# A dilated attention mixer ordered by head pairs

## What is computed

```python
proj = (h @ w_in).reshape(B, S, 3, 3, 16, 64)      # 3 groups, each q, k, v of 16 heads
for gi, (window, dilation) in enumerate(((128, 1), (512, 4), (2048, 16))):
    q = rms_norm(proj[:, :, gi, 0], g_q[gi]); k = rms_norm(proj[:, :, gi, 1], g_k[gi])
    s = q . k * 64 ** -0.5 + bias_table[bucket(pos_k - pos_q)]     # -inf outside the window
    lse = logsumexp(s); o = exp(s - lse) @ v
wts = softmax(lses over the 3 groups)
y = sum(wts * o) @ w_o
x = x + gate1 * y
```

## Time and profile before

| | us |
|---|---|
| median of 3 runs | 2215.91 |
| the profiled execution | 2213.28 |
| its span, first to last instruction | 2211.5 |
| PE busy | 2029.5 (92%) |
| DVE busy | 1458.9 (66%) |
| ACT busy | 1085.9 (49%) |
| POOL busy | 172.1 (8%) |
| mean granted PE clock | 0.953 |

### The profile page before, as it was taken

How to read it: one execution, slowest core, us unless ns; L and a number is a source line. 1 busy time by engine, 2 the same in 40 slices (tenths; PEclk the granted TensorE clock), 3 DMA queues, 4 the chain that set the end, 5 groups by cost and what they waited for, 6 DMA issues and landing times.

```text
span 2211.5 us, 34384 instructions
## 1 busy us (share of the span) xinstructions
PE 2029.5 (92%) x14140; PEld 1868.4 (84%) x14140; DVE 1458.9 (66%) x2577; ACT 1085.9 (49%) x1674; POOL 172.1 (8%) x243
## 2 busy tenths in 40 slices
PE   2758999889999998999889989999999879999998
PEld 1746999789898978999888889999999767888886
DVE  6696885666766556754765553888886696555554
ACT  3544553325665144543555445444444695444444
POOL 3020000000000000000000000000000492000000
PEclk7879999889999699999999999999999999999999
DMA  6534687526554014665433434555555203555553
GB/s 263 188 124 153 202 283 249 172 75 212 199 173 157 20 39 143 193 189 181 162 126 120 139 114 162 185 186 191 182 184 188 96 1 125 190 190 186 187 190 124
DMA packets 97084, 356.22 MB, mean 161 GB/s; under 512 B 10704, under 2 KB 10832, under 8 KB 96544
## 3 DMA queue, kind: packets, MB, share of 16 engines
q1 hardware_dynamic: 83824, 305.04, 41.1%
q0 software_dynamic: 12672, 48.08, 7.0%
q10 hardware_dynamic: 432, 0.90, 0.1%
HBM read 352.93 MB, written 1.05 MB: 160 GB/s over the span
## 4 chain that ended last, share of the span: by engine, by line
PE 79%; DVE 14%; ACT 4%; DMA 1%; issue 1%; SPq 0%; POOL 0%; DVEq 0%; ACTq 0%
PE psum L386 22%; PE psum L387 22%; PE psum L388 22%; PE psum L379 12%; DVE C L1432 2%; PE psum L393 1%; DVE wl L1460 1%; DVE araw L1443 1%; DVE one L1432 1%; ACT work L945 1%; DVE one L1437 1%; DVE work L1440 1%; DMA first<-in_ada_w 1%; ACT sqh L945 0%; DVE first L1443 0%
## 5 line engine op out<-in xcount | busy, mean ns | idle before, releaser
L1460 DVE TENSOR_TENSOR wl<-raw,wh 128x1024 fp32r<-128x1024 f32 (+1 forms) x564 | 686.7, 1223 | 469.8 <-ACT wh L957 468.7
L957 ACT ACTIVATE wh<-raw 128x1024 fp32r<-128x1024 f32 (+1 forms) x564 | 593.0, 1053 | 461.2 <-PE psum L388 444.7
L386 PE MATMUL psum<-peer_hh,wh 128*128 128x256 f32 x1152 | 325.9, 283 | 4.1 <-DVE peer_hl L1432 4.0
L387 PE MATMUL psum<-peer_hl,wh 128*128 128x256 f32 x1152 | 324.9, 282 | 0.0
L388 PE MATMUL psum<-peer_hh,wl 128*128 128x256 f32 x1152 | 324.9, 282 | 0.0
L386 PEld LDWEIGHTS psum<-peer_hh,wh 128*128 128x128 f32 x1152 | 218.2, 189 | 5.4 <-issue 4.4
L387 PEld LDWEIGHTS psum<-peer_hl,wh 128*128 128x128 f32 x1152 | 218.4, 190 | 0.0
L388 PEld LDWEIGHTS psum<-peer_hh,wl 128*128 128x128 f32 x1152 | 218.3, 189 | 0.0
L386 PE MATMUL psum<-wh,csh 128*128 128x512 f32 x512 | 202.5, 396 | 0.0
L387 PE MATMUL psum<-wl,csh 128*128 128x512 f32 x512 | 202.5, 395 | 0.0
L388 PE MATMUL psum<-wh,csl 128*128 128x512 f32 x512 | 202.5, 395 | 0.0
(11 more groups left out here) (422 smaller groups left out, 4589.2 us busy)
## 6 DMA issues: line engine op xcount, KB each, us to landing
raw<-in_mlp_w SPq DMA_DIRECT2D x128, 512.0 KB, 4.2
raw<-in_eu SPq DMA_DIRECT2D x128, 512.0 KB, 3.2
raw<-in_ev SPq DMA_DIRECT2D x128, 512.0 KB, 3.2
araw<-in_ada_w POOLq DMA_DIRECT2D x80, 512.0 KB, 4.2
raw<-in_dil_qk SPq DMA_DIRECT2D x48, 512.0 KB, 4.1
raw<-in_dil_v SPq DMA_DIRECT2D x24, 512.0 KB, 4.4
first<-in_ada_w SPq DMA_DIRECT2D x8, 1024.0 KB, 18.2
raw<-in_w_in SPq DMA_DIRECT2D x16, 512.0 KB, 3.3
```

The lines of the kernel that those rows point to most:

```text
L386: e.matmul(o, l[0], r[0], start=start, stop=False, skip_group_check=loose)
L387: e.matmul(o, l[0], r[1], start=False, stop=False, skip_group_check=loose)
L957: e.activation(b.wh[v % NSPLIT][:, 0:cols], b.raw[v % NRAW][:, 0:cols], ACT.Copy).then_inc(S.hi, 1)
L1460: e.tensor_tensor(b.wl[v % NSPLIT][:, 0:cols], b.raw[v % NRAW][:, 0:cols], b.wh[v % NSPLIT][:, 0:cols].bitcast(F32), ALU.subtract).then_in ...
```

## The change

The order of all engines is one list, `DIL_ORDER`, from which `PLAN` takes its units too.

- The value units come first, 18 of 24 (those for heads 0 to 11), and both bias tables are made beside them; `B` holds both tiles, and the mask is loaded in one piece.
- Then the q and k units in eight rounds, one for each pair of heads c: six units (q and k of three groups), so that a bank holds q and k of one group. `qk` keeps two rounds.
- The norm of round c is split: squares, sums and means in the round; the three reciprocal roots together one round later, after unit 3 (`root`), with the root squares and DVE's refining and scaling after units 3 and 4. DVE scales q and k separately, 256 columns each.
- The four attention steps of pair c-2 stand in round c, two after unit 0 and two after unit 1. `work` has three score buffers and one for transposed probabilities; in a step PE does `s3` before `s2`, and ACT the copy before the exponential.
- The last six value units follow round 7, beside the last scalings. Steps 24 and 25 come after them, steps 26 to 34 between the first six units of the output projection.
- The output projection goes by rows: unit i takes slice i of the attention output and adds to all eight column blocks in four banks, so it can begin when pair 0 is done; the residual is added after the last unit's blocks, and the four squares and sums follow.
- Modulation steps: one after every fourth of the 18 value units, then three in each round and in the late values (31 in all; before, every fourth unit and every third attention step).

```diff
+def dil_order():
+    values = [("dil_v", 8 * g + x, x // 2) for g in range(3) for x in range(8)]
+    out = []
+    for i, e in enumerate([e for e in values if e[2] < 3]):
+        out.append(e)
+        if i % 4 == 3:
+            out.append(("tick", 0, 0))
+    out.append(("biased", 0, 0))
+    late = [e for e in values if e[2] == 3]
+    def beside(c, z):
+        if z % 2 == 0:
+            s, g = (c, z // 2 - 1) if z else (c - 1, 2)
+            if 0 <= s < 8:
+                out.append(("sum", s, g))
+        s, g = {3: (c, 0), 5: (c, 1), 0: (c - 1, 2)}.get(z, (-1, 0))
+        if c and z == 3:
+            out.append(("root", c - 1, 0))
+        if c and z in (3, 4):
+            out.append(("root square", c - 1, z - 3))
+        if c and z == 4:
+            out.append(("root square", c - 1, 2))
+        if 0 <= s < 8:
+            out.append(("mean", s, g))
+        if z % 2 and c < 8:
+            out.append(("square", c, z // 2))
+        if z in (0, 2, 3):
+            out.append(("tick", c, z))
+        if c and z in (3, 4):
+            out.append(("scale", c - 1, z - 3))
+        if c and z == 4:
+            out.append(("scale", c - 1, 2))
+        for u in {0: (4 * c - 8, 4 * c - 7), 1: (4 * c - 6, 4 * c - 5)}.get(z, ()):
+            if 0 <= u < 24:
+                out.append(("step", u, 0))
+    for c in range(8):
+        for z in range(6):
+            out.append(("dil_qk", 8 * z + c, z))
+            beside(c, z)
+    for z in range(6):
+        out.append(late[z])
+        beside(8, z)
+    out += [("step", 24, 0), ("step", 25, 0)]
+    tail = [(26,), (27,), (28, 29), (30, 31), (32, 33), (34,), (), ()]
+    for i, steps in enumerate(tail):
+        out += [("step", u, 0) for u in steps] + [("dil_w_o", i, 0)]
+    return out
...
 # ScalarE
+            elif kind == "root":
+                ac.wait_ge(S.act, n[0])
+                if i:
+                    ac.wait_ge(S.dve, at["dqk", "out", i - 1, 2])
+                for g in range(3):
+                    act(m.hrs[:, g, :], m.hms[:, (3 * i + g) % 4, :], ACT.Abs_reciprocal_sqrt, mark=("root", i, g))
...
 # VectorE
+        def head_norm(c, g):
+            sq, ms, y = m.hrq[g], m.hms[:, (3 * c + g) % 4, :], m.hrs[:, g, :]
+            ve.wait_ge(S.act, at["head rs0", c, g])
+            stt(sq, ms, -0.5, sq, ALU.mult, ALU.mult)
+            own()
+            stt(sq, sq, 1.5, y, ALU.add, ALU.mult)
...
+            for x, gain in enumerate(("dil_g_q", "dil_g_k")):
+                z = slice(256 * x, 256 * x + 256)
+                stt(m.qk[:, c % 2, 2 * g + x, :], ps[:, z], vc(b, gain, g), sq[:, z], ALU.mult, ALU.mult,
+                    mark=("dqk", "out", c, g))
...
 # TensorE, the output projection
+        def rows(i):
+            if i == 0:
+                for c2 in range(4):
+                    take("dil_o", c2)
+            j = weights("dil_w_o", i)
+            pe.wait_ge(S.dve, at["dil", "out", i])
+            for c in range(8):
+                o = b.psum[:, at["bank", "dil_o", c // 2], (c % 2) * 256:(c % 2) * 256 + 256]
...
+        for c2 in range(4):
+            give("dil_o", c2, sem=S.dve, key=("dil_o", "out", c2))
+            square_sums("dil_o", c2, m.work)
```

More of the change, by code:

```diff
@@ L145, in plan @@
     add("mlp_w2", 32)
[L146 to L149, removed]
+    for kind, i, j in DIL_ORDER:
+        if kind in ("dil_v", "dil_qk", "dil_w_o"):
+            add(kind, 1, first=i)
     add("mlp_w1", 32, first=32)
@@ L686, in dilated @@
         phase("dil")
[L687 to L731, removed]
-                give("dv", g, c2, sem=S.act, key=("dv", "out", g, c2))
@@ L770, in s3, with step @@
                    mark=("dil", "pv", u) if kb == 3 else None)
[L771 to L777, removed]
+            if u % 4 == 3:
+                give("do", c, sem=S.dve, key=("dil", "out", c))
+        def step(i):
             if i < 32:
                 s1(i)
+            if 0 <= i - 3 < 32:
+                s3(i - 3)
@@ new lines, in dilated @@
+        for kind, i, z in DIL_ORDER:
+            if kind == "dil_v":
+                values(i, z)
+                next(side, None)
+            elif kind == "biased":
+                for _ in side:
+                    pass
+            elif kind == "dil_qk":
+                c = i % 8
+                if z % 2 == 0:
+                    take("dqk", c, z // 2)
+                ps = b.psum[:, at["bank", "dqk", c, z // 2], (z % 2) * 256:(z % 2) * 256 + 256]
+                j = weights("dil_qk", i)
+                for k in range(8):
+                    mm3(ps, wsp(j, k * 128, 128), sp(m.hh, k), k == 0, k == 7, unit=k == 7)
+            elif kind == "sum":
+                head_sums(i, z)
+            elif kind == "scale":
+                give("dqk", i, z, sem=S.dve, key=("dqk", "out", i, z))
+            elif kind == "step":
+                step(i)
+            elif kind == "dil_w_o":
+                rows(i)
@@ L1156, in dilated @@
         _, shift = shift_gain(b, 1, 0)
-        norm_x("n2", ("mlp0", 2), shift, m.hh, m.work[:, 0:2048], m.work[:, 2048:2816])
+        norm_x("n2", ("mlp0", 2), shift, m.hh, m.work[:, 0:2048], m.vtf[:, 0:768])
         ac.wait_ge(S.dve, at["tab diff"])
         act(m.tabs[0], m.ot[:, 0:192], ACT.Copy, mark=("tabs", "hi"))
[L1160 to L1200, removed]
@@ L1218, in mixer2 @@
+        for c2 in range(4):
+            square("dil_o", c2, m.work, ("dil_o", "out", c2))
     def mixer2():
@@ L2208, in modulation @@
                 yield
+            groups[0] = first + count
             yield
+    groups = [16]
     mods = modulation()
@@ L2218, in tick, with mod_until @@
                 next(mods, None)
+    def mod_until(first):
+        while groups[0] <= first:
+            next(mods)
     def lows(tag, m):
```

261 lines of the change are left out of this document (162 added, 99 removed).

## The result

The changed kernel took 2177.95 us (median of 4 runs, 2176.93 to 2178.57) against 2215.23 for the one before on the same chip (4 runs, 2213.45 to 2216.1): ratio 0.9832, 95% interval 0.9815 to 0.9849. The forecast was 2179, its range 2163 to 2199. The profiled execution took 2178.34 us with a span of 2176.5.

What follows compares the result with a forecast made beforehand. PE bounds the mixer, partly at half clock: 795.0 + 9 + 2 + 1 + 6.6 + 2 = 815.6, + 8.8 = 824.4 instead of 861.3; 36.9 less gives 2176.4 profiled, 2179 us median, range 2163 to 2199.

Steps and rivals of the forecast that it cites:

- first mixer matmul to first bias matmul: Mixer start: first comparison comes one 1.2 us operation sooner, so bias work starts at 426.7; before, PE waited until 427.85.
- clock in the bias stage, and the seam: Bias tables beside eighteen value units: 9 us lost to half clock (bounds 0 and 16), 2 waiting after the last group.
- rounds 0 to 7: Query and key rounds: 1 us of waits for rounds 0 and 1, 6.6 for rounds 2 to 7 (bounds 0 and 18).
- late values and tail: After the rounds: round 8 needs no new wait; copies in the three last steps cost 2 us, bounds 1 and 5.
- last output issue to the MLP: Mixer end: adds start within the last unit, 8.8 us in all, 7.2 before; over 9 would show it wrong.
- PE's sum: Whole mixer at full clock: units, bias matmuls, head sums and steps total 368.3 us; last output matmul issued at 795.0.
- queue walk: Rounds 2 to 7: following engine queues showed tight places within 0.5 us, charged 1.1 us a round.
- Table loads: ACT in rounds and end: a load costs 1.28 us; the skill's extra drain, estimated at 10 us more, was not added.
- B: Rival for the whole mixer: nothing exposed, no clock dip or queue wait, 20.6 us less, 2158; chance 0.13.
- C: Rival in the attention: each of twelve step pairs waits 2 us for DVE or ACT, 2196; chance 0.14.
- D: Rival in the bias stage: value units and bias groups run at 1.2 GHz throughout, slower at 2251; chance 0.05.
- E: Rival, no change: shorter clock loss is given back by attention waits of 3.6 us a pair, 2215; chance 0.02.

Runs made afterwards that it cites:

- second profile: Profile of the changed kernel run once more with no edit: 2177.43 us, ratio 0.9837 to the kernel before; mixer 407.2 us.
- late24: Changed kernel with attention steps 24 and 25 moved after the first late value unit instead of after all six: 2176.73 us, ratio 0.9827 to the kernel before.
- scale_early: Changed kernel with the last round's roots and scalings two late value units earlier, its means first: 2178.92 us, ratio 0.9841 to the kernel before.
- table_early: Changed kernel with the reciprocal root's table loaded before the four residual squares: 2178.96 us, ratio 0.9833 to the kernel before.
- steps4: Changed kernel with all four attention steps of a round behind unit 0, instead of two and two: 2180.64 us, ratio 0.9839 to the kernel before.
- bias1_alone: Changed kernel with the second bias table made in one piece after the eighteenth value unit, no units beside it: 2193.84 us, ratio 0.9905 to the kernel before.

## Why the prediction was right, step by step

The reason held: PE bounds the mixer, its work is unchanged, and what goes is PE work at half clock and, at the first table, waits. Of the terms I read the measured ones from the first profile of the changed kernel; the three in the middle are time beyond PE's work at full clock.

| term | forecast | measured | from |
|---|---|---|---|
| first mixer matmul to first bias matmul | 9.3 | 9.1 | 421.60 to 430.73 |
| clock in the bias stage, and the seam | 9 + 2 | 4.5 | 430.73 to 521.25 is 90.5 for 384 x 0.110 + 16 x 2.82 = 87.4; three units behind it 9.80 for 8.5 |
| rounds 0 to 7 | 1 + 6.6 | 2.4 | 531.05 to 743.7 is 212.7: five rounds of 30.6 for 30.2 of work, 59.7 for 59.3 in the first part |
| late values and tail | 2 | 8.0 | 743.7 to 813.97 is 70.3 for 13 units and 25.6 of steps, 62.3 |
| last output issue to the MLP | 8.8 | 10.6 | 813.85 to 824.41 |

*PE's sum.* Right, to the rounding: 0.110 a bias matmul (32 in 3.52), 2.67 a step, 2.82 a unit, and some 0.1 more at each change of kind. (A unit behind transposes takes 3.05 from start to start, but the transposes ahead of it only 0.41 instead of 0.59: 3.46 for 3.41.)

*The bias stage.* The mechanism was right, the 9 too much for this execution. In the second profile another 10.2 us of the stage ran at half clock, and the mixer took 4.4 more, so that there the term is 8.9 of the 11. It is no fixed number: the same code has it at 4.5 in one profile and near 9 in five. The wait for evacuations went, as forecast: no such row is left.

*The rounds.* The queue walk found four places within 0.5 us and charged 1.1 a round. The waits show none of them; what is seen of it is 0.16 in the second pair (its values take 1.18 instead of 1.02). In PE's order of time (the second pair of a round, to be laid beside the earlier trace rows) the values start at 663.97 and the transposes 1.17 later, where the first step of the pair has 1.02:

```profile
661.29 1.09 PE L442 MATMUL psum<-work,vt 128*64 128x128 f32 x8
662.31 0.66 PE L456 MATMUL psum<-con,work 128*128 128x128 f32 x4
662.90 1.14 PE L442 MATMUL psum<-qk 64*128 64x256 f32 x6
663.97 1.09 PE L442 MATMUL psum<-work,vt 128*64 128x128 f32 x8
665.14 0.66 PE L456 MATMUL psum<-con,work 128*128 128x128 f32 x4
```

The rest of the 0.4 a round is in the changes of kind. ACT and DVE were busy 20.7 and 23.0 of 30.6 (forecast 21.9 and 23.4). Where two chains meet within half a microsecond on paper, 0 was the better estimate.

*The tail, the step that failed.* I wrote that round 8 has no steps and needs no new wait. It has the last pair's norm chain on DVE, and I did not walk that queue on into step 24 and 25: the wait of 3.0 is there, it is followed by half clock (766.1 to 772.9: 3.0 lost over those rows), and of the copies that no scores hide only one shows, at 0.8. The other 1.2 are changes of kind and small waits. late24 and scale_early showed that the wait's place moves and that its cost stays.

*The end.* 1.8 over, beyond the 9 that the prediction named as the sign of a wrong end. I had let the adds begin inside the last unit. DVE had the low half for a unit of the MLP in front of them, which itself waited for ACT's high half (811.39), so that the adds began at 813.62 and the squares at 814.52. A mixer's last step shares its queue with the next stage's first weights, and I had counted only the former. The load between third and fourth square cost what was forecast, 1.28, and table_early took 1.17 of it back.

*Table loads.* After the load at 817.08 the next operation starts at 818.37, 0.01 behind its end, as in the earlier trace rows. The Trainium skill (ScalarE: Activation LUTs, "What ACT_TABLE_LOAD costs") adds a drain of about 1.38 us to every switch; by it the end would shorten by some 2.7 with the load out of the way, an estimate from that page. It shortened by 1.17, so here the measurement decides against the drain, and the term that I left at nothing stays at nothing.

*Why the number came out within 2 us.* In large part by chance. For the first profile the errors are -0.2 (start), -6.5 (bias), -5.2 (rounds), +6.0 (tail), +1.8 (end) and +4.2 (a later begin of the mixer), which with rounding, and 0.1 counted both in the tail and in the end, come to 0.0 at the MLP's first matmul (824.41, forecast 824.4). The second profile needs less luck, but some: its mixer is 407.2 where 407.0 was forecast (417.4 to 824.4), with bias -2.1, rounds -5.2, tail +6.0 and end +1.8. Two misses of 5 to 6 us, waits expected in the rounds and none in the tail, cancelled each other.

*The rivals.* B (2158) expected that nothing is exposed; 14.9 of the 20.6 are. C (2196), chains exposed in each pair, falls by the waits and by steps4. D (slower, bias work and value units at half clock) falls by the clock of 0.94 to 1.00. E needed C. What no rival said, and my own text neither: that the new order of the attention shows no gain of its own without the tables. My expectation for it in the pair without tables was 3 to 9, and it was 2.5. Without the tables PE's waits within the mixer are 8.2 in the kernel before (2.8, 2.3, 1.6 and 1.5) and 5.7 in the changed one (the tail's 3.0, and 2.7 for ACT, most of it at the end); against that the changed one has 6.8 us at half clock in its late steps, and the one before 3.4 where its attention starts.

Which share of the 16.3 at the first table is clock and which is waits? The profile of the kernel before without its second table has both in that stretch:

```profile
427.20:512.00 84.80, 76.41 (x523) 72.13 (x521) 53.68 (x81) 27.97 (x38) 2.13 (x4) 0.86 0.31 100
```

Of PE's waits there, two groups are missing in the kernel before without both tables, 8.4 us:

```profile
PE psum L379 <- DVE B L1429: 5.8, 2, 3.5
PE psum L379 <- DVE step L1437: 2.6, 2, 1.6
```

The clock of 0.86 is some 24 us at half, at 0.45 each 10.7. Together that is 19.1, where the medians leave 17.7 over the matmuls' 21.1; the changed kernel has 1.4 over them (22.5) and none of these waits. So, as an estimate from these rows, about half of the 16.3 is waits and half is clock. A finer split stays open, since the clock of one stretch differs by up to 4.5 us between executions.

## What to carry to other kernels

When one engine bounds everything, look for the stretches in which it is busy at the lower rate before looking for idle time: small matmuls on their own were at half clock with no gap in 41 us, and the same matmuls between projection units ran at full clock. Price a large reordering by leaving the suspected work out of both kernels: with both tables gone, all the rest of this diff was worth 2.5 us. When a queue is walked, walk it through the last round and into the next stage's first weights, for there the misses were.

## What was new about the hardware

*Half clock without idle time.* bias1_alone's window has PE busy 41.00 of 41.00 us with matmuls of 64 and 128 columns, and a granted clock of 0.50 throughout; the 64 matmuls at the seam fell to half from 516.9 on, again without a gap. The Trainium skill (TensorE: Matmul & The Clock Gate, "Why this matters for your kernels") asks for no idle gaps between matmul bursts. That keeps no clock here: it is what PE executes, not only whether it waits. What of it decides (columns, the many weight loads, 64 and 128 in turn, or the DMA queues, which stand nearly idle in that window at a share of 0.01) was not tried.

*The same code, another clock.* In the mixer of the changed kernel the stretches at the lower level are 3.4 or 6.8 us long, and where they fall differs between executions: none in the bias stage of the first profile before the seam, two (at 429.1 and 439.4) in the second. Over the 14 profiles of this case the code ahead of the mixer, which none of them changes, took from 415.8 to 421.9 us and was at half clock for 76.9 to 90.6.
